# Mixture of experts after a two-block attention layer: one visit per expert with rows gathered by a one-hot matrix, instead of rows sorted by group, and the chunk transposes of gated linear attention as a step of their own

## The reference, cut to what matters

```python
def _gla(q, k, v, g_out, a_low, w_a2, b_a2, norm_g):    # 4 heads, chunks of 64 rows
    ...
    att = jnp.where(causal, jnp.einsum('bnihd,bnjhd->bnhij', q_dec, k_inv), 0.0)
    o_intra = jnp.einsum('bnhij,bnjhv->bnihv', att, vf)
    upd = jnp.einsum('bnjhd,bnjhv->nbhdv', k_end, vf)
    ...                                                  # state = decay * state + upd, chunk after chunk
    o_inter = jnp.einsum('bnihd,nbhdv->bnihv', q_dec, s_prev)

def _hier_moe(h, w_r1, b_r1, w_r2, b_r2, w_gate, w_up, w_down):
    g_sel = jnp.argmax(g_logits, axis=-1)                # one group of 4 for each row
    ...                                                  # softmax over the 4 experts of that group, the best 2 of them
    combine = jnp.sum(one_hot(expert_id, 16) * (g_w * top_p)[..., None], axis=1)
    hid = jax.nn.silu(jnp.einsum('nd,edf->nef', hf, w_gate)) * jnp.einsum('nd,edf->nef', hf, w_up)
    hid = hid * combine[..., None]
    out = jnp.einsum('nef,efd->nd', hid, w_down)         # D 1024, F 256
```

## Time and profile before

| | us |
|---|---|
| median of 3 runs | 1603.36 (1593.64 to 1605.26) |
| the profiled execution, its own time | 1605.55 |
| span of its trace, first to last instruction | 1603.70 |
| mean granted TensorE clock | 0.953 of 2.4 GHz |
| gather matmuls (`resort`) begin | 1250.28 |
| first visit begins / last down product ends | 1270.3 / 1576 |
| last instruction | 1603.7 |

### The profile page before, as it was taken

How to read it: one execution, slowest core, us unless ns; L and a number is a source line. 1 busy time by engine, 2 the same in 40 slices (tenths; PEclk the granted TensorE clock), 3 DMA queues, 4 the chain that set the end, 5 groups by cost and what they waited for, 6 DMA issues and landing times. The chain is left out here.

```text
span 1603.7 us, 18670 instructions
## 1 busy us (share of the span) xinstructions
PE 1458.8 (91%) x6868; PEld 1130.4 (70%) x6868; DVE 650.1 (41%) x1411; ACT 711.3 (44%) x1192; POOL 539.1 (34%) x243
## 2 busy tenths in 40 slices
PE   5999888989899997999899999999999897989887
PEld 4777665457677765757677777888878776767665
DVE  2285453444510134358953332324222543333333
ACT  4542325234533556444456556354224443444451
POOL 3265111003252412324222242224342354445440
PEclk9999998789999998999999999999999898999898
DMA  4222111003552301312211232213432454554522
GB/s 143 87 80 78 40 40 34 22 14 105 171 161 66 105 27 43 89 53 79 85 54 59 62 102 67 73 53 99 151 105 90 133 184 158 171 158 149 178 90 99
DMA packets 98445, 150.74 MB, mean 94 GB/s; under 512 B 11919, under 2 KB 46917, under 8 KB 98341
## 3 DMA queue, kind: packets, MB, share of 16 engines
q1 hardware_dynamic: 95248, 144.59, 28.9%
q10 hardware_dynamic: 2804, 4.72, 1.0%
q0 software_dynamic: 288, 0.02, 0.0%
HBM read 143.01 MB, written 6.29 MB: 93 GB/s over the span
## 5 line engine op out<-in xcount | busy, mean ns | idle before, releaser
L824 POOL TENSOR_TENSOR w_lo<-raw,w_hi 128x1024 fp32r<-128x1024 f32 (+2 forms) x166 | 396.0, 2400 | 877.3 <-ACT w_hi L1533 844.2
L873 PE MATMUL ps<-w_hi,act_hi 128*128 128x512 f32 (+1 forms) x560 | 233.5, 417 | 7.5 <-POOL w_lo L824 5.9
L1533 ACT ACTIVATE w_hi<-raw 128x1024 fp32r<-128x1024 f32 (+1 forms) x174 | 175.4, 1034 | 113.8 <-PE ps L875 112.2
L874 PE MATMUL ps<-w_lo,act_hi 128*128 128x512 f32 (+1 forms) x560 | 221.3, 395 | 0.0
L875 PE MATMUL ps<-w_hi,act_lo 128*128 128x512 f32 (+1 forms) x560 | 220.3, 393 | 0.0
L873 PE MATMUL ps<-w_hi,mix_hi 128*128 128x512 f32 x432 | 181.3, 420 | 8.6 <-DVE mix_lo L2121 6.4
L874 PE MATMUL ps<-w_lo,mix_hi 128*128 128x512 f32 x432 | 171.4, 397 | 0.0
L875 PE MATMUL ps<-w_hi,mix_lo 128*128 128x512 f32 x432 | 171.2, 396 | 0.0
L873 PEld LDWEIGHTS ps<-w_hi,act_hi 128*128 128x128 f32 (+1 forms) x560 | 105.6, 189 | 48.1 <-issue 13.4
L875 PEld LDWEIGHTS ps<-w_hi,act_lo 128*128 128x128 f32 (+1 forms) x560 | 105.4, 188 | 25.5
L874 PEld LDWEIGHTS ps<-w_lo,act_hi 128*128 128x128 f32 (+1 forms) x560 | 105.7, 189 | 24.0 <-issue 1.7
(11 more groups left out here) (497 smaller groups left out, 2604.2 us busy)
## 6 DMA issues: line engine op xcount, KB each, us to landing
raw<-in_w_in SPq DMA_DIRECT2D x92, 512.0 KB, 3.6
raw<-in_w_out SPq DMA_DIRECT2D x16, 512.0 KB, 3.5
raw<-in_w_mem_kv SPq DMA_DIRECT2D x16, 512.0 KB, 4.7
raw<-in_w_gate SPq DMA_DIRECT2D x32, 256.0 KB, 3.1
raw<-in_w_up SPq DMA_DIRECT2D x32, 256.0 KB, 3.9
raw_more<-in_w_down SPq DMA_DIRECT2D x16, 512.0 KB, 4.1
raw_more<-in_w_gate SPq DMA_DIRECT2D x32, 256.0 KB, 3.3
raw_more<-in_w_up SPq DMA_DIRECT2D x32, 256.0 KB, 4.0
```

Of the source, the lines that this page charges most:

```text
L824: pool.tensor_tensor(lo[:, 0:a], raw_slot(g)[:, 0:a], hi[:, 0:a].bitcast(F32), ALU.subtract).then_inc(*POOL.done(("w_lo", g)))
L873: pe.matmul(dst, l_hi, r_hi, start=start, stop=False, skip_group_check=skip)
L874: pe.matmul(dst, l_hi, r_lo, start=False, stop=False, skip_group_check=skip)
L1533: nc.scalar.activation(split_slot(g)[0][:, 0:a], raw_slot(g)[:, 0:a], ACTF.Copy).then_inc(*ACT.done(("w_hi", g)))
```

## The change

Experts: `sort` now ranks rows within each expert. `route(0)` also finds the two experts (`hot`, 128x16 for each tile), 10 small matmuls add up the ranks, and `so` is the rank or zero. For a pair of experts `perm` is four 128x256 one-hot pieces. Every pair has its own gather (64 matmuls of 256 columns), its own small product for the shares, two groups of four transposes of `perm`, and its own share of the scatter back (`unsort`: 8 jobs, each of 4 matmuls of 512 columns for a pair, added to `x1`). Each expert is visited once, with up to 128 rows. There are no flags for visits. One flag, set by three short DVE operations behind the first pair's `combine_s` and read by PE there, by DVE and ACT at the end, guards a dense path (`overflow`) for rows past 128 of an expert, for all 16 experts and 4 tiles. The gather of pair p+1 is interleaved with the odd expert of pair p (for the first pair with both), the scatter with the next even expert. Four raw slots and eight split slots remain, `x1` stays in place, POOL subtracts 5 of 6 units, and `y_exp` is gone: the down product is scaled and split by ACT and DVE straight from PSUM. GLA: the transposes and scores are a step `gla_turn` that stands earlier in the list.

```diff
-E_SLOTS = 12
+E_SLOTS = 8
...
-    order += [x for h in (0, 1) for x in (("gla_states", h), ("gla_values", h))]
-    order += fill[:4] + [("gla_decays", 2)] + fill[4:8] + [("gla_rstd", 0)] + fill[8:12] + [("gla_decays", 3)] + fill[12:]
-    order += [x for h in (2, 3) for x in (("gla_states", h), ("gla_values", h))]
+    order += [("gla_turn", 0), ("gla_states", 0), ("gla_turn", 1), ("gla_values", 0), ("gla_states", 1), ("gla_values", 1)]
+    order += fill[:4] + [("gla_decays", 2)] + fill[4:8] + [("gla_rstd", 0), ("gla_decays", 3)] + fill[8:12] + [("gla_turn", 2)] + fill[12:]
+    order += [("gla_turn", 3), ("gla_states", 2), ("gla_values", 2), ("gla_states", 3), ("gla_values", 3)]
...
-    order += [("route", 0), ("sort",), ("weights", 4), ("route", 1), ("resort",), ("combine_s",), ("weights", E_UNITS)]
-    for v in range(NT * N_EXP):
-        order += [("visit", v)]
-        if v >= NT and v // NT % 4 == 0:
-            order += [("finish", v - NT)]
-        order += [("weights", E_UNITS * (v // NT + 1) + (2, 3, 4, 6)[v % NT])]
-    order += [("finish", NT * (N_EXP - 1) + s) for s in range(NT)]
-    order += [("unsort",)]
+    order += [("route", 0), ("sort",), ("weights", 4), ("perm", 0), ("route", 1)]
+    order += [("resort", 0, i) for i in range(4)] + [("combine_s", 0)] + [("permT", 0, j) for j in range(2)]
+    order += [("perm", 1), ("weights", 8)]
+    for e in range(N_EXP):
+        pair = e // 2
+        gather = [("combine_s", pair + 1)] + [("resort", pair + 1, i) for i in range(4)]
+        turns = [("permT", pair + 1, j) for j in range(2)]
+        if e < 2:
+            jobs = [gather, turns][e]
+        elif e == N_EXP - 1:
+            jobs = [("unsort", e - 1, 1, t, n) for n in range(2) for t in range(NT)]
+        elif e % 2:
+            jobs = gather + turns
+        else:
+            jobs = [("unsort", e - 2, 2, t, n) for t in range(NT) for n in range(2)]
+        at = (len(jobs) + 1) // 2
+        wanted = [("weights", E_UNITS * e + 9 + i) for i in range(4)]
+        order += [("up", e), wanted[0]] + jobs[:at - 1] + [wanted[1]] + jobs[at - 1:at] + [("turn", e), wanted[2]]
+        order += jobs[at:] + [wanted[3], ("down", e), ("weights", E_UNITS * e + 14)]
+        if e % 2 and e < N_EXP - 3:
+            order += [("perm", pair + 2)]
+    order += [("overflow",)] + [("unsort", N_EXP - 1, 1, t, n) for n in range(2) for t in range(NT)]
...
+        jobs = [step for step in order if step[0] in ("combine_s", "resort", "permT", "unsort")]
+        job_bank = {step: (2, 3, 7)[i % 3] for i, step in enumerate(jobs)}
...
-            return DVE if g == router_unit or g >= expert_unit and (g - expert_unit) % E_UNITS >= 4 else POOL
+            return DVE if g == router_unit or g >= expert_unit and (g - expert_unit) % E_UNITS == 5 else POOL
...
-                        pool.wait_ge(*DVE.after("combine"))
+                        pool.wait_ge(*DVE.after("so"))
...
@@ tensor @@
+            def resort(pair, i):
...
+                claim(bank, (DVE, ("s_lo", pair, 2 * i + 1)))
+                for k in (2 * i, 2 * i + 1):
+                    _, cols = pair_half(pair, k)
+                    for t in range(NT):
+                        for x in (xs_hi, xs_lo):
+                            mm = pe.matmul(ps[:, bank, cols], x[:, t, P * k:P * k + P], perm[:, t, :],
+                                           start=(t == 0 and x is xs_hi), stop=(t == NT - 1 and x is xs_lo), skip_group_check=True)
...
+            def turn(e):
+                pe.wait_ge(*DVE.after("hid", e))
+                claim(4, (DVE, ("hid_lo", e)))
...
+            def down(e):
+                pe.wait_ge(*DVE.after("hid_lo", e))
...
+                    claim(5 + n, (DVE, ("y_lo", e, n)))
...
+            def unsort(e0, count, t, n):
...
+                for e in range(e0, e0 + count):
+                    pe.wait_ge(*ACT.after("permT", e // 2, e % 2))
+                    pe.wait_ge(*DVE.after("y_lo", e, n))
...
@@ scalar @@
+            def down(e):
...
+                for n in range(2):
+                    act.wait_ge(*PE.after("down", e, n))
+                    nc.scalar.activation(y_hi[:, e % 2, 512 * n:512 * n + 512], ps[:, 5 + n, :], ACTF.Copy,
+                                         scale=combine_s[:, e // 2 % 2, e % 2, e:e + 1]).then_inc(*ACT.done(("y_hi", e, n)))
...
@@ vector @@
+            def turn(e):
...
+                dve.tensor_copy(hid_hi[:, e % 2, :], ps[:, 4, 0:D_EXP]).then_inc(*DVE.done(("hid_hi", e)))
+                dve.wait_ge(*DVE.after("hid_hi", e))
+                dve.scalar_tensor_tensor(hid_lo[:, e % 2, :], ps[:, 4, 0:D_EXP], 1.0, hid_hi[:, e % 2, :].bitcast(F32),
+                                         ALU.mult, ALU.subtract).then_inc(*DVE.done(("hid_lo", e)))
```

More of the change, by code:

```diff
@@ L1296, in sort @@
                 pe.wait_ge(sort_in, 32)
[L1297 to L1306 removed]
+                claim(6, (DVE, ("so",)))
@@ new lines, in sort @@
+                for t in range(NT):
+                    cols = slice(N_EXP * t, N_EXP * (t + 1))
+                    mm = pe.matmul(ps[:, 6, cols], before_t[:, :], hot[:, t, :], start=True, stop=(t == 0), skip_group_check=True)
+                    for b in range(t):
+                        mm = pe.matmul(ps[:, 6, cols], all_ones[:, :], hot[:, b, :], start=False, stop=(b == t - 1), skip_group_check=True)
+                mm.then_inc(*PE.done(("ranks",)))
+                claim(4, (DVE, ("most",)))
@@ L1325, in flag @@
-            def flag(v):
-                return active[NT * (v // NT // 4) + v % NT]
-            def skip(done, steps):
-                pe.matmul(ps[0:1, 7, 0:1], ones[:, 0:1], ones[:, 0:1], start=True, stop=True).then_inc(done[0], steps)
-            def down(v):
-                e, s = divmod(v, NT)
-                g0 = expert_unit + E_UNITS * e + 4
-                b0 = 5
-                pe.wait_ge(*DVE.after("w_lo", g0 + 1))
-                pe.wait_ge(*DVE.after("hid_lo", v))
-                claim(b0, (DVE, ("y", v)))
-                claim(b0 + 1, (DVE, ("y", v)))
+                    pe.wait_ge(*DVE.after("perm", pair, t))
@@ new lines, in down @@
+                    mm.then_inc(*PE.done(("unit", g), ("down", e, n)))
+            def unsort(e0, count, t, n):
+                bank = job_bank["unsort", e0, count, t, n]
+                claim(bank, (DVE, ("x", e0, t, n)))
+                for e in range(e0, e0 + count):
+                    pe.wait_ge(*ACT.after("permT", e // 2, e % 2))
+                    pe.wait_ge(*DVE.after("y_lo", e, n))
+                    turned = permT[:, e // 2 % 2, e % 2, P * t:P * t + P]
+                    cols = slice(512 * n, 512 * n + 512)
+                    pe.matmul(ps[:, bank, :], turned, y_hi[:, e % 2, cols], start=(e == e0), stop=False)
+                    mm = pe.matmul(ps[:, bank, :], turned, y_lo[:, e % 2, cols], start=False, stop=(e == e0 + count - 1))
+                last = t == NT - 1 and n == 1
+                mm.then_inc(*PE.done(("unsorted", e0, t, n), *[("spent", e) for e in range(e0, e0 + count) if last]))
@@ L2495, in route @@
                 g = rl[:, :, 0:4]
-                if part == 0:
-                    dve.wait_ge(*DVE.after("rl"))
-                    return first_best(g, 0, 1, 3, ("hot",))
-                dve.tensor_tensor(four(2), g, one(0), ALU.subtract).then_inc(*DVE.done(("r_g",)))
                 e4 = rl[:, :, 4:20].rearrange("p t (g e) -> p t e g", g=4)
@@ L2598, in visit @@
-            def visit(v):
-                e, s = divmod(v, NT)
-                with dve.If_ne(flag(v), 0):
-                    if e % 4:
-                        hid_low(v - NT)
-                    dve.wait_ge(*ACT.after("e_silu", v))
-                    if v >= NT:
-                        dve.wait_ge(*PE.after("turn", v - NT))
-                    done = DVE.done(("hid", v))
-                    dve.tensor_tensor(hid[:, s, :], ps[:, s, D_EXP:2 * D_EXP], e_silu[:, :], ALU.mult).then_inc(*done)
-                    if e % 4:
-                        done = add(v - NT)
-                with dve.Else():
-                    skip(0, v, done, 3 if e % 4 else 1)
@@ L2613, in hid_low @@
-            def hid_low(v):
-                dve.wait_ge(*ACT.after("hid_hi", v))
-                dve.scalar_tensor_tensor(hid_lo[:, v % NT, :], ps[:, 4, 0:D_EXP], 1.0, hid_hi[:, v % NT, :].bitcast(F32),
-                                         ALU.mult, ALU.subtract).then_inc(*DVE.done(("hid_lo", v)))
-            def finish(v):
-                with dve.If_ne(flag(v), 0):
-                    hid_low(v)
-                    done = add(v)
-                with dve.Else():
-                    skip(1, v, done, 2)
+                dve.wait_ge(*PE.after("ranks"))
@@ new lines, in most_rows @@
+            def most_rows():
+                dve.wait_ge(*PE.after("counts"))
+                dve.tensor_reduce(most[:, 0:1], ps[:, 4, 0:N_EXP], X, ALU.max).then_inc(*DVE.done(("most",)))
+                dve.wait_ge(*DVE.after("most"))
```

(3 more changed lines are left out.)

598 lines of the change are left out of this document (319 added, 279 removed).

## The result

The changed kernel takes 1576.62 us (median of 4 runs, 1570.75 to 1578.60), the kernel before, beside it, 1604.31 (1593.64 to 1606.66). The ratio is 0.9852, with a 95% interval of 0.9811 to 0.9892: 28 us faster, where 59 were forecast. 1576.6 lies inside the range (1531 to 1582) and 32 us above the forecast. Measured again, on another chip with more runs: 1569.04 against 1596.45, ratio 0.9831 (0.9793 to 0.9870).

A forecast was written before the change was run, and what follows sets the result against it. No engine was full in the visits; 70 us there were PE waiting or slow. First `up` at 1268.6, plus 265.7 of PE work, less 3.6, plus 4.0, plus 12.7, less 3 for GLA: span 1544.4, rounded to 1545 (1531 to 1582).

The forecast's parts named there:

- PE's work from the first `up`: TensorE's sum over the experts: visits 134.7, seven further pairs' gather, shares and transposes 72.8, scatter 58.2, together 265.7 us.
- rival B: Narrow gather matmuls of 256 columns cost load plus stream, 0.22 us each, +45: 1590, no change; chance 0.07.
- rival C: The experts' weight feed through four raw slots sets the pace; at 3.6 us a unit 1624, slower; chance 0.06.
- D: An expert has over 128 rows and the dense path runs: over 2000 us; chance 0.02 with the like.
- The tail: After the last `down`: y's parts, DVE's flag and jump (2 us), 8 sums and the store, 12.7 us.
- The small stalls: PE's uncovered waits in the experts: 1.5 us in expert 1 and 2.5 us in expert 15.
- Linear attention: GLA heads 2 and 3: splitting off transposes and scores shortens a bare wait, 3 us off (0 to 9).
- 8 gather parts and 4 `perm` pieces of about 0.42: Part of DVE's work for a pair of experts, each about 0.42 us, within some 20 us of 34.5.
- PE asks for them a whole even expert later: On DVE, `perm` pieces fall behind an odd expert's y parts; PE needs them only a whole even expert later.
- rival A: Experts: ACT's list or DVE's sums late, most of 32 turns and downs wait 1.1 us; +35, 1580; chance 0.14.
- the first gather: Ahead of the first `up`: half as long as before, matmuls at 0.121 us, paying for the longer routing.
- The flag: Ahead of the first `up`, PE waits about 1.2 us for it, plus a register load of 1.5 (0 to 3).

The follow-up runs named there:

- e1: The changed kernel with the positions copied once into PSUM, where every `perm` piece reads them in place of SBUF: 1537.83 us, ratio 0.9632 to the kernel before.

## Why the prediction was wrong

**What held.** 16 products; PE's work from the first `up` (265.7 us forecast; e1, without the waits, has the last `down` 264.9 us after the first `up`, where 266.1 were forecast). Matmuls of 256 columns cost 0.12 us (1276.49 to 1276.61 and so on in the trace after), so rival B is out. ACT waited some 20 us for landings in the experts, but PE has no wait for a low part of a weight there, so rival C is out. D wasn't taken. The tail took 12.9 us (12.7 forecast). The small stalls were forecast as 4.0 (1.5 in expert 1, 2.5 in expert 15) and measured 2.0 (1.1 and 0.9). Linear attention: 3 forecast, 0 to 9 measured.

**The step that failed** is the term "8 gather parts and 4 `perm` pieces of about 0.42". The 0.42 was read from the earlier trace rows, `hid<-ps,e_silu`, which has one input in PSUM; a piece has both in SBUF, and stands beside POOL, which I had counted as busy for 24.2 of 34.5 us. It measured 2.0 to 2.2 us in pairs 0 and 2 to 7 (7.87 and 8.0 to 8.85 for four). With it fell the sentence that hid it: "PE asks for them a whole even expert later". That is true of `perm`, but on DVE's queue behind the pieces stand `hid` and the scatter sums of the even expert, and PE asks for these at once. It was the very case of an instruction whose own result is early and whose neighbours are late. So this was rival A's place (DVE's sums late) with a cause that it didn't name, in six of 16 experts, once for 4.8 us (7.1 in the repetition) and five times for 2.6, where A had 1.1 at most of 32 places. A's total of 1580 lies near the measured time, but not by A's mechanism.

**The account.** The profiled span of 1568.9 is 24.5 above the forecast 1544.4: 21.2 from the first `up` to the end (300.0 for 278.8), 7.2 from `hot` to the first `up` (26.7 for 19.5), less 3.9 because `hot` came earlier than counted, at 1242.2 for 1246.1 (1249.1 and the 3 of linear attention). The first `up` stood at 1268.9, where the forecast had 1268.6, or 1265.6 with the 3 us of linear attention taken off: the two errors there cancel in part. Of the 7.2 at the front 6.4 are the pieces again (8.15 us from `so` to the first gather matmul, 1.7 forecast). 2.0 are the first gather, 9.8 us in place of 7.8: the granted clock is 0.50 from 1242.2 to 1254, where PE ran small matmuls and then waited 6.7 us, and the gather's matmuls come 0.21 us apart until 1259.7 and 0.12 behind, where the forecast had priced all of them at 0.121. The flag cost 1.3 less than counted. The profiled run was the fastest of four; the median is 5.9 above it, where the forecast had taken 2.2 below. With the 1.85 us around the span, less the 0.6 by which 1545 lies above 1544.4, that is the 32.

**The sign was there.** The trace of the kernel before has 32 subtractions of 128x1024 on DVE in this stretch, which I priced as "1.2 to 1.9" without asking why. Four of them, by source line:

```profile
L2642 DVE TENSOR_TENSOR gap_w<-raw,gap_w x4: 1211/1584/3243, 1287.2 to 1532.1; 128x1024 fp32r<-128x1024 f32 x4
```

One form, one size, 1.21 to 3.24 us: something held it. The one of 3.24 started at 1287.16, while POOL's subtractions ran from 1284.59 to 1289.32; 1.1 us behind their end it was done. Its neighbour with a PSUM input, is 0.747 each time. And the old `perm`, 1.67 us for four of 512 columns, ran while POOL waited for `combine`.

## What to carry to other kernels

Price a DVE instruction by its operands' places as well as by its size: with two inputs in SBUF, or in the copy and scalar forms out of SBUF, it waits for the GpSimd subtraction that runs, once each (beside fills, which read nothing, the two-input form didn't). Where GpSimd works back to back, many short DVE instructions are the worst case; move one operand to PSUM, merge them, or let GpSimd wait for them: it had room. And when a step moves onto a queue with time to spare, ask what stands behind it there, not only who waits for its result.

## What the runs showed of the hardware

- The wait behaves as a lock held for one GpSimd instruction: 128x256 with two SBUF inputs 0.42 us alone, 2.56 beside subtractions of 2.40; a PSUM input 0.42 in both; the scalar form 0.28 and 2.38; a copy 0.29 and 2.43; 128x16 0.17, and up to 2.31 for every second one. Beside fills of 0.95 us: 0.42, and 1.11 for the copy.
- A jump over a block that isn't executed took DVE 2.7 to 3.0 us ahead of its next instruction, wherever the flag was loaded.
- Kernels with the same instructions up to the routing reached the `ranks` matmuls at 1231.3 to 1246.5 us. From 300 to 360 us the granted clock was 0.83 in the changed kernel's profile and 0.94 in e1's. Differences of a few us between medians of four runs say nothing here. A stretch of the profile that leaves that part out says more, but it too came out 2.0 and 2.5 us apart for the same kernel.
